# Column blocks of x in one piece for each load, and the first expert's rows gathered as columns in PSUM

## The reference

```python
h = rmsnorm(x, norm_mix_g)
x = x + hybrid_mixer(h, w_in, ...)          # convolution and gated linear attention, then w_out
h = rmsnorm(x, norm_ffn_g)
logits = h @ w_router + b_router            # 32 experts
top_v, top_i = top_k(logits, 4); gates = softmax(top_v)
for each expert e, for the tokens that chose e:
    gu = h_tok @ w_gate_up[e] + b_gate_up[e]           # 1024 x 2048
    act = (clip(up) + 1) * min(gate, 7) * sigmoid(1.702 * gate)
    y[tok] += gate_weight * (act @ w_down[e] + b_down[e])   # 1024 x 1024
out = rmsnorm(x + y, norm_final_g)
```

## Time and profile before

| | |
|---|---|
| median of 3 runs | 1042.41 us (1041.95 to 1043.14) |
| the profiled execution | 1042.84 us |
| its span, first to last instruction | 1041.1 us |
| mean granted TensorE clock | 0.998 |
| PE busy | 1009.0 us, 97% |
| moved by DMA | 423.86 MB, mean 407 GB/s |

### The profile page before, as it was taken

One profiled execution on the slowest core, in us unless ns is written; L12 is line 12 of the kernel. 1 busy time (PEld: TensorE's weight loads), 2 busy tenths in 40 slices (PEclk: granted clock), 3 DMA queues, 4 the chain that ended last, 5 costly groups with the idle time before them and its releaser, 6 DMA issues.

```text
span 1041.1 us, 12117 instructions
## 1 busy us (share of the span) xinstructions
PE 1009.0 (97%) x4824; PEld 412.3 (40%) x4824; DVE 245.0 (24%) x625; ACT 140.8 (14%) x281; POOL 6.5 (1%) x24
## 2 busy tenths in 40 slices
PE   8999999999999999999999999999999999999996
PEld 7688843333333333333333333333333333333333
DVE  2264132112122222222221122221212121122122
ACT  1100121111111111111111111111111111111112
POOL 1000000000000000000000000000000000000000
PEclk9999999999999999999999999999999999999999
DMA  9983789999999999999999999999999999999995
GB/s 367 408 369 134 311 343 422 387 426 423 420 435 429 429 434 429 434 429 434 429 428 436 431 433 429 429 434 429 436 428 434 429 428 436 426 427 427 426 421 222
DMA packets 23270, 423.86 MB, mean 407 GB/s; under 512 B 2888, under 2 KB 3408, under 8 KB 5840
## 3 DMA queue, kind: packets, MB, share of 16 engines
q1 hardware_dynamic: 22320, 422.45, 95.6%
q10 hardware_dynamic: 928, 1.09, 0.3%
HBM read 422.48 MB, written 1.05 MB: 407 GB/s over the span
## 4 chain that ended last, share of the span: by engine, by line
PE 79%; DMA 19%; issue 1%; DVE 0%; ACT 0%; SPq 0%; DVEq 0%; PEldq 0%
PE bank L1503 33%; DMA ring<-in_w_expert 19%; PE bank L1523 18%; PE bank L1243 5%; PE bank L1389 5%; PE y L1566 4%; PE bank L1541 3%; PE y L1352 2%; PE bank L1227 1%; PE bank L1445 1%; PE bank L1218 1%; PE bank L1352 1%; PE bank L1547 1%; PE bank L1624 1%; DMA h_t<-in_x_cols 1%
## 5 line engine op out<-in xcount | busy, mean ns | idle before, releaser
L1503 PE MATMUL bank<-ring,x_t 128*64 128x512 f32 x1984 | 447.1, 597 | 0.0
L1523 PE MATMUL bank<-ring,act 128*64 128x512 f32 x992 | 230.5, 596 | 14.2 <-DMA ring<-in_w_expert 14.2
L1503 PEld LDWEIGHTS bank<-ring,x_t 128*64 128x64 f32 x1984 | 133.9, 136 | 261.9 <-issue 257.1
L1523 PEld LDWEIGHTS bank<-ring,act 128*64 128x64 f32 x992 | 68.4, 137 | 145.2 <-issue 144.5
L1076 DVE TENSOR_TENSOR gu_b<-bank,bias_t 128x512 f32<-128x512 f32 x64 | 44.2, 691 | 330.3 <-PE bank L1541 330.2
L704 ACT COPY gu_sb<-bank 128x512 f32<-128x512 f32 x64 | 37.4, 585 | 222.6 <-PE bank L1503 222.6
L1566 PE MATMUL y<-z,p_t 64*128 64x512 f32 x248 | 61.6, 615 | 0.0
L1389 PE MATMUL bank<-x_sb,p_row 128*64 128x512 f32 x256 | 60.6, 593 | 0.0
L1029 DVE TENSOR_TENSOR x_t<-bank,cols 128x512 f32<-128x512 f32 x30 | 20.7, 691 | 164.9 <-PE bank L1445 164.9
L1243 PE MATMUL bank<-h_t,ring 128*128 128x256 f32 x256 | 56.1, 380 | 0.0
L1015 DVE TENSOR_SCALAR p_row<-slot,rank,rstd 128x64 f32<-128x64 f32 x62 | 16.7, 311 | 165.1 <-PE bank L1547 165.1
(11 more groups left out here) (231 smaller groups left out, 403.2 us busy)
## 6 DMA issues: line engine op xcount, KB each, us to landing
ring<-in_w_expert SPq DMA_DIRECT2D x72, 4096.0 KB, 36.1
ring<-in_w_expert SPq DMA_DIRECT2D x36, 2048.0 KB, 47.4
ring<-in_w_expert SPq DMA_DIRECT2D x18, 1024.0 KB, 10.7
ring<-in_w_in SPq DMA_DIRECT2D x5, 2048.0 KB, 25.1
ring<-in_w_out SPq DMA_DIRECT2D x2, 2048.0 KB, 26.9
ring<-in_w_expert SPq DMA_DIRECT2D x4, 512.0 KB, 5.6
ring<-in_w_down_last SPq DMA_DIRECT2D x4, 512.0 KB, 25.3
ring<-in_w_down_last SPq DMA_DIRECT2D x2, 1024.0 KB, 24.6
```

What stands on the lines that cost most here:

```text
L1503: ins = mm(bank[h][a * SLOTS:(a + 1) * SLOTS, :], x_t_of(it)[:, k, :], w[:, kk, a, :], start=k == 0, stop=k == KT - 1)
L1523: ins = mm(bank[0][a * SLOTS:(a + 1) * SLOTS, :], act_of(it)[:, k, :], w[:, kk, a, :], start=k == 0, stop=k == KT - 1)
```

## The change

**Loads of x by columns.** In HBM `x_cols` was one array in which a partition's 8 KB held k 0 to 7, and each of the two loads read 4 KB out of every 8 KB. Now it is two arrays of 128 x 4 KB, one for each load, each of them 512 KB in one piece. Destination, size and place in SP's queue stay.

**Item 0's input.** The new `gather_first` makes `x_t`'s form at once: for each k the stationary operand is the 128x128 block of `xs` and the moving one is `p_row` (64 columns), so that the result is features by slots. It lies in `bank[2]` (k 0 to 3) and `bank[3]` (k 4 to 7). ACT's two copies to `x_row` and PE's four transposes of item 0 go. DVE's two multiplications stay, each now over four neighbouring k; the first stands ahead of the reciprocal of the gates' sum, the second behind the gates. Tile 0's products fill the places of one `idle(2)` and of the old `gather([0])`, and two of them stand ahead of the last transposes of tile 1. The other `idle(2)` and the `idle(1)` between the item's transposes go, and `turn_all_gates` (the two transposes of `gates4`, L1458) moves behind item 0's `turn_gates`. The second half of `x_t` is waited for at k 3, no longer at k 2.

```diff
-                sp.dma_start(h_t[:, r, :], x_cols.rearrange("p (k t) -> p k t", k=KT)[:, r, :]).then_inc(s_xc[i], 16)
+                sp.dma_start(h_t[:, r, :], x_cols[i].rearrange("p (k t) -> p k t", k=KT // 2)).then_inc(s_xc[i], 16)
...
-            for f in range(2):
-                act_e.wait_ge(s_xg, 1)
-                act_e.copy(x_row[:, f * 256:(f + 1) * 256], bank[3][:, f * 256:(f + 1) * 256]).then_inc((s_xr_a, s_xr)[f], 1)
...
+            def keep_first(i):
+                dve.wait_ge((s_xT_a, s_xT)[i], 1)
+                k = slice(i * KT // 2, (i + 1) * KT // 2)
+                dve.tensor_tensor(x_t[:, k, :], bank[2 + i][:, 0:KT // 2 * SLOTS].rearrange("p (k s) -> p k s", s=SLOTS),
+                                  cols[:, COL_FFN:COL_FFN + KT].rearrange("p (k s) -> p k s", s=1)[:, k, :]
+                                  .broadcast_to([P, KT // 2, SLOTS]), ALU.mult).then_inc((s_xt_a, s_xt)[i], 1)
+            keep_first(0)
             link(dve.reciprocal(ngt[:, :], ngt[:, :]))
             dve.tensor_tensor(gates[:, :, :], ex[:, :, :],
...
             dve.wait_ge(s_gtk, 1)
+            keep_first(1)
...
+            def gather_first(t, k0, k1):
+                for k in range(k0, k1):
+                    f = k % (KT // 2)
+                    ins = mm(bank[2 + k // (KT // 2)][:, f * SLOTS:(f + 1) * SLOTS], xs[:, t, k * P:(k + 1) * P], p_row[:, t, :],
+                             start=t == 0 and f == 0, stop=t == TT - 1 and f == KT // 2 - 1, skip_group_check=True)
+                    if t == TT - 1 and f == KT // 2 - 1:
+                        ins.then_inc((s_xT_a, s_xT)[k // (KT // 2)], 1)
...
             logits(1, 4, 6)
+            pe.wait_ge(s_p0, 1)
+            gather_first(0, 0, 2)
             transpose_x(1, 6, 8, 5)
-            idle(2)
+            gather_first(0, 2, 5)
             pe.wait_ge(s_trD, 1)
             logits(1, 6, 8)
-            pe.wait_ge(s_p0, 1)
             mm(bank[5][:, E:2 * E], ones[:, :], chosen[:, 0, :], start=True, stop=False)
-            gather([0])
+            gather_first(0, 5, KT)
...
             idle(1)
             pe.wait_ge(s_p0, 2)
-            gather([1])
-            idle(2)
+            gather_first(1, 0, KT)
...
-                    idle(1 - i)
+            def turn_all_gates():
                 pe.wait_ge(s_gtk, 2)
...
-                    if isinstance(it, int) and it == 0 and k == 2:
+                    if isinstance(it, int) and it == 0 and k == 3:
                         pe.wait_ge(s_xt, 1)
...
                 turn_gates(it)
+                if known == 0:
+                    turn_all_gates()
                 gate_up(it, 1, range(4))
...
-    laid["x_cols"] = np.asarray(inputs["x"])[0].T.reshape(KT, P, T).transpose(1, 0, 2).reshape(P, KT * T)
+    laid["x_cols"] = np.asarray(inputs["x"])[0].T.reshape(2, KT // 2, P, T).transpose(0, 2, 1, 3).reshape(2, P, KT // 2 * T)
```

More of the change, by code:

```diff
@@ L359, in build @@
         s_xg = sem("x_gathered")
-        s_xr_a = sem("first_x_row_half_ready")
         s_xT_a = sem("first_x_half_turned")
@@ L685, in _ @@
             act_e.activation(ex[:, :, :], ex[:, :, :], ACT.Exp).then_inc(s_le, 1)
-            for f in range(2):
-                act_e.wait_ge(s_xg, 1)
-                act_e.copy(x_row[:, f * 256:(f + 1) * 256], bank[3][:, f * 256:(f + 1) * 256]).then_inc((s_xr_a, s_xr)[f], 1)
             act_e.preload_act_table_set("sigmoid_and_others")
             def keep_gathered(it):
-                act_e.wait_ge(s_xg, it + 1)
+                act_e.wait_ge(s_xg, it)
                 act_e.copy(x_row[:, :], bank[3][:, :]).then_inc(s_xr, 1)
@@ L1034, in _ @@
                             .broadcast_to([P, TT, SPLITS, E])).then_inc(s_gtk, 1)
[L1035 to L1041, removed]
             place_gates(0, slot1[:, :])
@@ L1436, in _ @@
             pe.wait_ge(s_p0, 2)
-            gather([1])
-            idle(2)
+            gather_first(1, 0, KT)
             nb = BLOCKS - 1
             def turn_gathered(it):
-                pe.wait_ge(s_xr, it + 1)
+                pe.wait_ge(s_xr, it)
                 for f in range(4):
@@ L1446, in turn_gathered @@
                 ins.then_inc(s_xT, 1)
[L1448 to L1452, removed]
-                        ins = nc.tensor.transpose(bank[(2, 4)[i]][:, f % 2 * P:(f % 2 + 1) * P], x_row[:, f * P:(f + 1) * P], ident[:, :])
-                    ins.then_inc((s_xT_a, s_xT)[i], 1)
-                    idle(1 - i)
+            def turn_all_gates():
                 pe.wait_ge(s_gtk, 2)
@@ L1460, in turn_first @@
                 ins.then_inc(s_gt, 1)
-            turn_first()
             def count_extras():
```

## The result

The changed kernel takes 1045.05 us (median of 22 runs, 1040.98 to 1046.40), the kernel before beside it 1042.76 us (22 runs, 1041.95 to 1043.45). The ratio is 1.0017 [1.0011, 1.0023]: slower by 2.3 us in the medians. The whole interval lies above 1, though 0.17% is just inside the 0.2% that I had named as the bound of what can be told. The forecast was 1041.7 with a range up to 1043.0, so it missed.

The account below looks back on a forecast made before the run. PE's work before 204 us sets the transfers' restart and so the end; 0.38 (gather) + 0.4 (layout), about 0.8 us off 1042.84, gave 1042.0, adjusted for the runs' median and caution to 1041.7 us, range 1040.6 to 1043.0.

Parts of the forecast that it names:

- the fourth rival: In the new gather's stretch PE's clock falls to half, item 0's first chunk taking 3.58 us more: 1045.3 us; chance 0.05.
- the last three products of tile 0: Narrow gather products placed in PE's wait for tile 1's top four, where the old gather stood: claimed to cost nothing.
- What bounds the kernel: PE's gain or loss before 204 us moves SP's issue, the transfers and the end one for one; later waits stay unchanged.
- The gather's price: Each PE record of the new narrow gather products, two records a product, was claimed to take 0.115 us.
- the third rival: The gather's narrow products cost more, the gain gone at 0.13 us a record: 1042.3 to 1043.6 us; chance 0.12.
- Item 0's first product: After the new gather, the first expert item's start on PE: claimed at 139.42 instead of 140.02 us, 0.60 us earlier.
- what is left after the gates' transposes: Gain of the new gather from item 0's second chunk on, once 0.22 us of transposes come back: 0.38 us.
- The layout's 0.4 us: At the kernel's first loads, x by columns in contiguous pieces lets PE's first projection finish 0.4 us earlier, ends 0 and 1.4.
- The second block of DVE: Sign for the layout: DVE's second four multiplications start near 8.1 us or earlier; at 8.5 the layout did nothing.
- The second rival: The layout does nothing because first loads are slow by position; 0.1 to 0.4 us left, 1042.0 to 1042.3 us; chance 0.20.

Follow-up runs that it names:

- experiment 4: The kernel before with all its idle products removed and the wide gather kept: 1042.92 us, ratio 1.0004.
- experiment 3: The changed kernel with three idle products put into PE's wait for tile 1's top four: 1042.50 us, ratio 0.9992.
- experiment 5: The kernel before with only the new gather (old layout of x) and three idle products in PE's wait for tile 1's top four: 1042.47 us, ratio 0.9998.
- experiment 9: The changed kernel with three idle products in PE's wait for tile 1's top four, repeated in another job: 1042.53 us, ratio 0.9997.
- experiment 10: The changed kernel with two idle products in PE's wait for tile 1's top four: 1042.58 us, ratio 0.9997.
- experiment 1: The kernel before with only the new layout of x by columns: 1042.52 us, ratio 0.9998.
- experiment 7: The changed kernel with three idle products ahead of tile 1's logits of k 4 and 5, outside the wait: 1045.78 us, ratio 1.0026.
- experiment 8: The changed kernel with one more of tile 0's gather products moved into the wait, four instead of three: 1045.16 us, ratio 1.0020.
- experiment 6: The changed kernel with one idle product in PE's wait for tile 1's top four: 1045.50 us, ratio 1.0016.
- experiment 2: The changed kernel with the old layout of x by columns, so the new gather alone: 1044.63 us, ratio 1.0012.

## Why the prediction was wrong

**The step that failed** is the fourth rival, "PE's clock falls", with the chance 0.05: its cost was kept out of the sum and out of the range, and it is what happened in 21 of 22 runs. The reason given against it, "more PE records than before stand in the stretch", counted the wrong thing, for there are more records and the clock falls. The safety was drawn from one row, a clock of 1.00 at 3.71 busy of 4 us, though that row was taken with the wide gather and the idle products in place; experiment 4 shows that the idle products did work, since without them 3 of 11 runs fall. Five of the six go, not "four of the five".

Ahead of that stands a wait that the prediction didn't work out: "the last three products of tile 0 fall into PE's wait for the choice [...] and cost nothing". The wide gather had left 0.13 us of this wait, the three narrow products leave 0.44. Experiments 3, 5, 9 and 10 fill exactly it, and no run falls. The rows before could have given its size: six records at 0.115 are 0.69 us, and a wide gather takes 1.08. That this would make a fall nearly certain no row of before says.

The Trainium skill, TensorE: Matmul & The Clock Gate, Part 1, has it that a clock at the full level is released by activity and not the default. I had quoted it and given it too little weight. The trace agrees with that sentence: 1.00 in the earlier trace rows, down to 0.50 behind a stretch with a bare wait in the windows above.

**The size of that rival** was made up differently than I wrote. I let all of the first chunk run at half, 3.58 us more. In fact the fall covers the gather (+1.64 us against experiment 3) and 3.25 of the chunk's 5.21 us (+1.63): 3.27 us together, for 3.58. That the rival's 1045.3 us lies near the measured 1045.05 is in part luck: it counts in 0.4 us of the layout that did not show and a price too high by 0.3, and the median mixes two sizes of fall.

**What bounds the kernel** was right. In the changed kernel the loss passes one for one (+3.28 by PE's chain, +3.28 at SP's issue, +3.5 in the span), and the waits after 690 us stay 14.2 us, eight of them. In experiment 3 chain and issue agree (-0.37 and -0.37), but the span is 1.0 us shorter, since those waits are 13.6 us there. So single spans scatter by some 0.6 us behind the issue, and a step of this size is read at SP's issue, not at the end.

**The gather's price** was right, where the clock holds. A record costs 2.00 / 16 = 0.125 us in experiment 3; I had taken 0.115. The break-even of 0.13, the third rival, is close but not reached. Item 0's first product is at 139.43 us instead of 140.02, 0.59 us earlier for 0.60 forecast, with the first 64 products done at 21.27 us in both traces; what is left after the gates' transposes is 0.37 on SP's issue, for 0.38. That both agree to 0.01 us is partly luck: the gather starts 0.06 us late where I had 0.17, and takes 2.00 us where I had 1.84.

**The layout's 0.4 us** did not show. The second block of DVE is at 8.38 and 8.40 us instead of 8.51, where 8.1 was wanted. The traces of all thirteen kernels tell more than the two above. With the new layout (eight traces) that block starts at 8.18 to 8.51 us, median 8.39; with the old one (five) at 8.51 to 8.84, median 8.67. So the second load of x is some 0.3 us faster, but it is no longer what PE waits for: its first product starts at 6.89 to 7.22 us instead of 6.25 to 6.58, with the weights' quarter. Its 64 products end at 21.02 to 21.75 us instead of 21.27 to 21.60, and without the four traces that begin slowly at 21.02 to 21.30 instead of 21.27 to 21.60. What the layout may be worth there, about 0.2 us by the middle of these, is less than single executions scatter. By medians experiment 1 is 0.47 us below its reference, with an interval that holds 1. The second rival's outcome came, its reason did not: the slow stretch isn't fixed by its position, since it moves from 2 to 4 us to 4 to 6 us with the layout. Why it lies where it lies was not tried.

The Trainium skill, Perfetto Trace Analysis, section Contiguity and DMAs, says that contiguity matters only within a partition's line. This case's time agrees, within the 0.1% that experiment 1 can tell. The windows don't agree altogether: with the new layout 2 to 4 us carry 278 to 327 GB/s instead of 213 to 237, which is lost again from 4 to 6 us (207 to 260 instead of 380 to 400).

**What is left of the change with the wait filled** (experiments 3, 9, 10) is 1042.50 to 1042.58 us against 1042.82 to 1042.99: 0.2 to 0.5 us by medians, where the accounts of the chain give 0.37. The intervals all reach 1, so a measurement can't tell it from the kernel before, nor from the layout alone (1042.52).

What stays open: which property of the stretch the chip judges by. The runs show that filling the wait decides, and that the new gather's stretch falls much more often than the old one's even with fewer waits. The sixteen records behind the wait aren't what brings the fall: it comes before the first of them in experiments 7 (137.6 us against 138.44) and 8 (136.4 against 137.77), and within 0.2 us of it in the other three traces. So what counts lies ahead of them; which of the narrow products there, no run separates. The runs don't show a rule.

## What to carry to other kernels

Wide products ahead of PE's waits, and idle products that stand in them, are part of the timing: when an edit takes them out or swaps wide products for narrow ones, look at PE's granted clock in windows of one microsecond, in many executions, before counting any saving. A busy share near one is no proof that the clock holds, and a clock of 1.00 measured with the old products in place says nothing about a kernel without them. If the clock falls, try idle products exactly in the wait that precedes the fall, enough to close it; here two did, and three at another place cost 0.64 us and cured nothing.

## What the runs showed of the hardware

- A wait of 0.44 us, in a stretch otherwise full of narrow products, is followed by 1.2 GHz in 21 of 22 runs of the changed kernel, and one of 0.17 us (experiment 6) in 8 of 12. The fall comes when PE is busy again: 0.3 us after the wait begins in experiment 8, 0.8 in experiment 7, 1.4 in experiment 6, 1.5 in the changed kernel and in experiment 2. In each of these five traces the clock is at 1.2 GHz for 6.8 us, worked out as above, with PE busy throughout.
- Three waits of 0.42 to 0.52 us in the stretch with the wide gather leave the clock at 1.00 in the profiled execution of experiment 4, and 8 of its 11 runs don't fall.
- Falls come in two sizes. In the changed kernel the eight runs at a mean clock of 0.996 have a median of 1043.7 us, the thirteen at 0.994 to 0.995 one of 1045.3. The shorter one was never caught in a profile; that it is about half as long is an estimate from the mean clock alone.
- At 1.2 GHz the narrow products take 3.64 / 16 = 0.23 us a record, at 2.4 GHz 0.125 (experiment 3), a factor of 1.8.
- The DMA engines are slow for two of the first eight microseconds whichever layout x has (213 GB/s from 2 to 4 us before, 240 from 4 to 6 in experiment 1), and carry 393 to 400 GB/s in the stretch behind it.
